# The factor of the MLP's norm moved into the last norm, and the residual's transposes and two up tiles moved in the order of PE

## What is computed

```python
def rmsnorm(x, g):
    x32 = x.astype(jnp.float32)
    y = x32 * lax.rsqrt(jnp.mean(x32 * x32, axis=-1, keepdims=True) + EPS)
    return y.astype(x.dtype) * g
...
        x = x + rmsnorm(merged @ w_out[l], post_norm_mix[l])
        h2 = rmsnorm(x, pre_norm_mlp[l])
        y = jnp.square(jax.nn.relu(h2 @ w_up[l])) @ w_down[l]
        x = x + rmsnorm(y, post_norm_mlp[l])
```

## Time and profile before

| | |
|---|---|
| Three runs | 1450.80, 1450.85, 1452.98 us; median 1450.85 |
| Span of the profiled execution | 1447.7 us (its own time is not given apart) |
| PE busy | 1319.0 us, 91% |
| DVE busy | 952.2 us, 66% |
| ACT busy | 493.1 us, 34% |
| POOL busy | 459.2 us, 32% |
| HBM | 274 GB/s over the span |

### The profile page before, as it was taken

One profiled execution on the slowest core, in us unless ns is written; L12 is line 12 of the kernel. 1 busy time (PEld: TensorE's weight loads), 2 busy tenths in 40 slices (PEclk: granted clock), 3 DMA queues, 4 the chain that ended last, 5 costly groups with the idle time before them and its releaser, 6 DMA issues.

```text
span 1447.7 us, 25101 instructions
## 1 busy us (share of the span) xinstructions
PE 1319.0 (91%) x9618; PEld 1240.8 (86%) x9618; DVE 952.2 (66%) x2094; ACT 493.1 (34%) x965; POOL 459.2 (32%) x325
## 2 busy tenths in 40 slices
PE   9999999999999896887878787879899999899997
PEld 8999999988889896887868787878886789789996
DVE  4689987665685775859585768755416447656665
ACT  5534456444133121212112221211225456434343
POOL 1587722000225554554545454546003000000000
PEclk9999999999999998898999999989999999999999
DMA  7555554553489999999999999999930134245552
GB/s 286 196 186 175 182 187 163 179 193 131 183 341 394 426 427 428 427 428 428 428 427 426 426 426 427 427 428 427 405 148 30 35 112 177 101 147 196 182 189 73
DMA packets 57896, 397.92 MB, mean 275 GB/s; under 512 B 6352, under 2 KB 9040, under 8 KB 10192
## 3 DMA queue, kind: packets, MB, share of 16 engines
q0 software_dynamic: 36864, 268.45, 44.1%
q1 hardware_dynamic: 20944, 128.28, 24.8%
HBM read 395.66 MB, written 1.05 MB: 274 GB/s over the span
## 4 chain that ended last, share of the span: by engine, by line
PE 57%; DMA 21%; DVE 11%; issue 7%; ACT 3%; POOL 1%; DVEq 0%; POOLq 0%; ACTq 0%
DMA rows_late<-peer_uv_dram,stage 21%; PE bank L745 11%; PE bank L746 11%; PE bank L747 11%; PE bank L1006 7%; PE bank L712 6%; PE bank L730 5%; DVE rows_late L2064 3%; ACT w_hi L1228 1%; POOL rows_late L654 1%; PE bank L867 1%; DVE w_lo L542 1%; PE bank L891 1%; PE bank L961 1%; PE bank L850 0%
## 5 line engine op out<-in xcount | busy, mean ns | idle before, releaser
L1006 PE MATMUL bank<-h_norm,rows_late 128*128 128x128 f32 x2816 | 327.8, 279 | 22.9 <-ACT h_norm L1417 22.9
L1006 PEld LDWEIGHTS bank<-h_norm,rows_late 128*128 128x128 f32 x2816 | 323.9, 195 | 26.0 <-ACT h_norm L1417 26.0
L2064 DVE SCALAR_TENSOR_TENSOR rows_late<-rows_late,squares 128x1024 f32<-128x1024 f32 x176 | 213.4, 1229 | 118.0 <-DMA rows_late<-peer_uv_dram,stage 107.9
L1006 PE MATMUL bank<-h_norm,rows_early 128*128 128x128 f32 x1280 | 174.3, 303 | 78.2 <-ACT h_norm L1417 78.2
L1006 PEld LDWEIGHTS bank<-h_norm,rows_early 128*128 128x128 f32 x1280 | 168.6, 217 | 84.1 <-ACT h_norm L1417 83.7
L654 POOL DMA_INDIRECT rows_late<-peer_uv_dram,stage x165 | 195.3, 1184 | 131.4 <-PE bank L1006 84.0
L542 DVE TENSOR_TENSOR w_lo<-raw,w_hi 128x2048 fp32r<-128x2048 f32 x66 | 151.3, 2294 | 100.5 <-ACT w_hi L1228 97.0
L1228 ACT ACTIVATE w_hi<-raw 128x2048 fp32r<-128x2048 f32 x94 | 178.9, 1904 | 56.4 <-PE bank L747 49.4
L745 PE MATMUL bank<-x_hi_a,w_hi 128*128 128x256 f32 x672 | 190.9, 284 | 2.7 <-DVE x_lo_a L1633 1.8
L746 PE MATMUL bank<-x_lo_a,w_hi 128*128 128x256 f32 x672 | 190.2, 283 | 0.0
L747 PE MATMUL bank<-x_hi_a,w_lo 128*128 128x256 f32 x672 | 190.1, 283 | 0.0
(11 more groups left out here) (353 smaller groups left out, 1886.1 us busy)
## 6 DMA issues: line engine op xcount, KB each, us to landing
raw<-w_in_dram SPq DMA_DIRECT2D x28, 1024.0 KB, 4.9
raw<-w_up_dram SPq DMA_DIRECT2D x16, 1024.0 KB, 4.9
raw<-w_down_dram SPq DMA_DIRECT2D x16, 1024.0 KB, 4.8
rows_late<-w_in_dram SPq DMA_DIRECT2D x10, 1024.0 KB, 12.7
raw<-w_kv_dram SPq DMA_DIRECT2D x8, 1024.0 KB, 4.9
rows_late<-w_peer_q_dram SPq DMA_DIRECT2D x5, 1024.0 KB, 11.8
raw<-sc_w_out_dram SPq DMA_DIRECT2D x4, 1024.0 KB, 4.9
raw<-cf_w_pw_dram SPq DMA_DIRECT2D x4, 1024.0 KB, 5.0
```

Source lines behind the costliest of these rows:

```text
L1006: mm = nc.tensor.matmul(ct(Y_ACC[c][t // 4], t % 4, P), expert_rows(k)[:, D + t * P:D + (t + 1) * P], ct(diag, k % DIAGS, P), start=False, ...
L2064: w_.scalar_tensor_tensor(out=row, in0=row, scalar=1.0, in1=h_tok[:, c * D:(c + 1) * D], op0=ALU.mult, op1=ALU.mult, accum_out=pre[:, side ...
```

## The change

Three things. First, the norm's factor r of a token leaves the up product. max(u, 0) without r, squared, is smaller by r², so is y, and the last norm divides it out again, save for its epsilon: y·r²/sqrt(mean(y²)·r⁴ + EPS) = y/sqrt(mean(y²) + EPS/r⁴). EPS/r⁴ is EPS·(m + EPS)² with m the mean square of the token. ACT computes it as one Square of the statistic (`up_eps`), and it stands as the bias where the last norm had EPS. The statistic is now taken by token, two single columns, with `squares` as the stationary operand. Square root, reciprocal and the multiplication by `rstd` are gone; `turns` is a plain max. Second, X stands behind U2 instead of ahead of D0, and ACT copies it out behind `hid_hi` 5 instead of 3. Third, U15 stands ahead of D13, and the list of loads ends up 13, down 12, up 14, up 15, down 13, down 14, down 15; the `w_hi` and `w_lo` of the last block come behind those of hidden tile 31. Three new columns (`eps_cubed_root`, `up_eps`) are allocated ahead of the large buffers, which lie 64 bytes further on.

```diff
@@ -80,6 +80,9 @@
+
+DOWN_BEHIND = {0: (), **{b: (b - 1,) for b in range(1, FH - 2)}, FH - 2: (), FH - 1: (FH - 3, FH - 2, FH - 1)}
@@ -155,11 +158,10 @@
         add("w_up_2", [b], "up", 2, "dve", 2 * b)
-        if b == 1:
+        if b == 2:
             other("xtok", 4, "act")
-        if b:
-            p.append(("w_down_2", b - 1, [], "dve"))
-    p.append(("w_down_2", FH - 1, [], "dve"))
+        for d in DOWN_BEHIND[b]:
+            p.append(("w_down_2", d, [], "dve"))
@@ -239,7 +241,7 @@
-SCALED = ("xa", "mlp")
+SCALED = ("xa",)
@@ -290,6 +292,8 @@
         eps_squared = sb("eps_squared", 1)
+        eps_cubed_root = sb("eps_cubed_root", 1)
+        up_eps = sb("up_eps", NC)
@@ -627,6 +631,7 @@
             g.memset(eps[:], EPS).then_inc(filled, 1)
+            g.memset(eps_cubed_root[:], EPS ** 1.5).then_inc(filled, 1)
@@ -782,7 +787,9 @@
                 pe.wait_ge(squared, square_count(name, k))
-                mm = nc.tensor.matmul(STAT[:, 0:SEQ], mean_d[:], ct(squares, k), start=(k == 0), stop=(k == DT - 1))
+                for c in range(NC):
+                    mm = nc.tensor.matmul(STAT[:, c:c + 1], ct(squares, k)[:, c * P:(c + 1) * P], mean_d[:, 0:1],
+                                          start=(k == c == 0), stop=(k == DT - 1 and c == NC - 1))
@@ -1158,21 +1165,32 @@
             linear("up", [3], "w_up_2", 1, "mlp", DT, 256, lo=P)
-            pe.wait_ge(residual_added, DT)
-            for n in range(4):
-                c, part = divmod(n, 2)
-                out = open_tile("xtok", n)
-                for j in range(4):
-                    mm = nc.tensor.transpose(out[:, j * P:(j + 1) * P], x_piece(c, 4 * part + j), ident)
-                mm.then_inc(acc_ready, 1)
-            pe.wait_ge(rooted, len(ROOTS))
-            for b in range(2, FH):
-                for f in (2 * b - 4, 2 * b - 3):
+            def down_pair(d):
+
+                for f in (2 * d, 2 * d + 1):
...
+
+            def x_by_token():
+
+                pe.wait_ge(residual_added, DT)
+                for n in range(4):
+                    c, part = divmod(n, 2)
+                    out = open_tile("xtok", n)
+                    for j in range(4):
+                        mm = nc.tensor.transpose(out[:, j * P:(j + 1) * P], x_piece(c, 4 * part + j), ident)
+                    mm.then_inc(acc_ready, 1)
+
+            pe.wait_ge(rooted, len(ROOTS))
+            for b in range(2, FH):
+                if b < FH - 1:
+                    down_pair(b - 2)
                 linear("up", range(2 * b, 2 * b + 2), "w_up_2", b, "mlp", DT, 256)
+                if b == 2:
+                    x_by_token()
+            down_pair(FH - 3)
@@ -1241,7 +1259,7 @@
                     if ROOTS[n - 1] in SCALED:
-                        wait_drained(act, {"xa": "q", "mlp": "up"}[ROOTS[n - 1]], 0)
+                        wait_drained(act, "q", 0)
@@ -1301,7 +1319,7 @@
-            act.wait_ge(filled, 6)
+            act.wait_ge(filled, 7)
@@ -1557,22 +1575,24 @@
             ahead("up", 0)
-            root("mlp")
+            act.wait_ge(stat_ready, NORM_AT["mlp"] + 1)
+            s.activation(up_eps[:], STAT[:, 0:NC], ACT.Square, scale=EPS ** 0.5, bias=eps_cubed_root[:, 0:1]).then_inc(rooted, 1)
...
                 s.activation(ct(hid_hi, f % FH), ct(hid, f % 4), ACT.Copy).then_inc(x_hi_ready, 1)
-                for n in range(4 if f == 3 else 0):
+                for n in range(4 if f == 5 else 0):
                     drain("xtok", n, ct(x_tok, n, 512), width=512)
-                round_to(LOAD_OF["up", 0] + f + 1)
+                round_to(LOAD_OF["up", 0] + f + (1 if f < 2 * FH - 2 else 0))
             act.wait_ge(acc_freed["act"], FREE_ORDER[TILE_AT["xtok", 3]][1])
+            act.wait_ge(rooted, len(ROOTS))
...
                 act.wait_ge(half_squared, c + 1)
-                s.activation(half_col[:, c:c + 1], sum_col[:, 2 * c:2 * c + 1], ACT.Identity, bias=eps[:, 0:1],
+                s.activation(half_col[:, c:c + 1], sum_col[:, 2 * c:2 * c + 1], ACT.Identity, bias=up_eps[:, c:c + 1],
@@ -2240,7 +2260,7 @@
             ahead("up", 0)
-            rstd_of("mlp")
@@ -2253,13 +2273,14 @@
                     dve.wait_ge(x_lo_ready, split_count("hid", f - 4))
-                dve.wait_ge(*freed(w_.scalar_tensor_tensor(out=turns[:], in0=acc("up", f), scalar=0.0,
-                                                           in1=rstd[:], op0=ALU.max, op1=ALU.mult)))
+                dve.wait_ge(*freed(w_.tensor_scalar(turns[:], acc("up", f), 0.0, None, ALU.max)))
...
                     hid_low(f - 1)
-                subtract_to(LOAD_OF["up", 0] + f + 1)
+                if f < 2 * FH - 2:
+                    subtract_to(LOAD_OF["up", 0] + f + 1)
             hid_low(2 * FH - 1)
+            subtract_to(len(LOADS))
```

## The result

| | us |
|---|---|
| before, median of 4 runs | 1450.82 (1449.55 to 1452.98) |
| changed, median of 4 runs | 1457.07 (1455.85 to 1457.46) |
| ratio, 95% interval | 1.0039 (1.0027 to 1.0052) |
| span of the profiled execution, changed | 1453.9 (its own time 1455.85) |

The changed kernel is 0.4% slower where 1447.4 was forecast. The last stage went as forecast; the loss stands ahead of it. Three marks, first before, then changed (PE timeline: start, us, instruction, idle before), show this: the first product behind the gather (`squares,rows_late`), the first up matmul (`x_hi_b,w_hi`) and the last matmul (`w_hi,hid_lo`). The other lines of the changed kernel are used further down.

A forecast was written before the change was run, and what follows sets the result against it. It took PE to bound the last stage, with DVE barely keeping up; -4.8 (reordering and norm factor) - 0.6 (end) + 2.0 (low clock) = -3.4 us took the span from 1447.7 to 1444.3, plus 3.15 gives 1447.4, range 1445.0 to 1450.3.

The forecast's parts named there:

- The step that failed: Large buffers, gather: 64 bytes off a multiple of 256 cost nothing, as `x_res` 383 and `cf_acc` 384 GB/s seemed equal.
- Rival (3): Gather: the 64-byte shift makes its packets 1% longer, costing 6.4 us, 1453.8 in all; chance 0.08.
- the rule named beside it: Skill's rule for descriptors off 256 bytes: 258 beats for 256 per 8 KB row, 0.8% on the gather, 1452.5 in all.
- The norm factor: Start of last stage: reciprocal goes, DVE's first run is 1.78 us earlier, plain max takes 0.42 us.
- D0 and U2 ahead of X: Start of last stage: first down pair at 1260.5, wait before fourth transpose group shrinks from 4.71 to 3.5 us; 4.8 gained.
- The clock: Behind the 3.5 us wait before the fourth transpose group: low PE clock costs 2.0 us, bounds 0 and 2.9.
- The statistic's new shape: PE, start of last stage: tile 3 ends at most 1.6 us later, hidden, costed at nothing.
- the two beats of 5.39: DVE, start of last stage: two tiles of 5.39 us put `turns` 5 at 1276.52.
- The end: Last pairs: wait for `hid_lo` (2.64 us) becomes one of 2.2 us for `w_lo`; 0.6 us gained.
- a possible loss of 1 to 1.7 us: Last pairs: if the wait at the end lowers PE's clock in a run, 1 to 1.7 us are lost.
- The sum of the stage: Last stage: -4.8 - 0.6 + 2.0 = -3.4 us.
- Rival (4): Last stage: reordering does nothing since PE waits for DVE anyway; only the reciprocal counts, -1.8 us, 1449.1; chance 0.06.

The follow-up runs named there:

- c5: Kernel before with only `rows_late`, `w_hi`, `w_lo` and other buffers behind the pad 64 bytes further on, `rows_early` aligned: 1447.70 us, ratio 0.9994.
- a4: Kernel before with `rows_early`, later small buffers and hid 64 bytes further on, `rows_late`, `w_hi` and `w_lo` unmoved: 1447.26 us, ratio 0.9990.
- c1: Kernel before with every large buffer 32 bytes past a multiple of 256: ratio 1.0080.
- c2: Kernel before with every large buffer 128 bytes past a multiple of 256: ratio 1.0082.
- d1: Kernel before with only `x_hi_a` and `x_lo_a` moved, 64 bytes further on: 1446.19 us, ratio 0.9965.
- d2: Kernel before with only `x_hi_a` and `x_lo_a` moved, 128 bytes further on: 1447.16 us, ratio 0.9978.
- d4: Changed kernel realigned to 256, residual transposes behind the second down pair, down 14 its own pair, both activation pairs 64 bytes further on: 1428.62 us, ratio 0.9843 to before.
- a2: Kernel before with all large buffers 64 bytes further on, nothing else: 1457.69 us, ratio 1.0059.
- b1: Kernel before with the new norm factor alone, both old orders kept, large buffers on multiples of 256: 1448.99 us, ratio 0.9986.
- c4: Changed kernel on multiples of 256 with the old order at the end: 1448.53 us, ratio 0.9982 to before.
- b2: Changed kernel on multiples of 256 with the residual transposes behind the second down pair: ratio 0.9933 to before.
- a1: Changed kernel with `row_pad` cut from 64 to 48, large buffers back on multiples of 256: 1442.92 us, ratio 0.9964 to before.
- a3: Kernel before with all large buffers 256 bytes further on: 1448.87 us, ratio 0.9999.

## Why the prediction was wrong, and where it was right

**The step that failed** is the one that set the 64 bytes aside: "So an offset of 64 bytes shows no cost, and a fixed price for a row would weigh eight times as much there as in the 8 KB rows of the gather." Its second half holds: the price of a packet is nearly fixed, 5.6 ns on 46.0 in rows of 1 KB and 4.3 ns on 309.1 in rows of 8 KB, so it weighs some nine times as much in the short ones. Its first half is what failed: the price isn't paid at once, and the window of the earlier trace rows from 3.70 to 4.90 us lies in the part of `x_res` that doesn't pay yet. The price begins only after a while (c5, a4, `cf_acc` in a4), and the gather, with nothing but rows off their multiple, pays nearly all the time. The trace of before already had it: at 5.10 to 5.70 us, where the last of `x_res` lands, it moved

```profile
5.10:5.70 0.60, 0.00 (x0) 0.00 (x0) 0.07 (x1) 0.60 (x3) 0.00 (x0) 1.00 1.13 359
```

359 GB/s. Other packets are mixed in there, but the 1 KB packets alone tell: they take 46.0 ns each from 3.4 to 4.9 us, and 51.7 from 5.2 to 5.8, the two values of `cf_acc` on its multiple and off it. One window inside a transfer doesn't tell its rate. Rival (3) had place and cause right, with a chance of 0.08; it was priced at 1% where 1.4% was measured, and the rule named beside it gave 0.8%. By that rule the price would double from 32 to 64 bytes and again to 128, and c1 and c2 show that it doesn't. Put in at the size of its packets, 8.9 us, the forecast would have been 1447.4+8.9 = 1456.3 against 1457.07. That this comes so close is in part luck, as the next sum shows.

**Of the 10.05 us** ahead of the stage 7.8 are the gather (from 367.42 to 1047.54, 680.12 us, before; 369.65 to 1057.59, 687.94, now). 2.2 arose in the first 30 us of the profiled execution, and no term of the sum had them. They are the clock's. The trace records 1.00 from 4.00 us before, 0.50 from 7.41 and 1.00 again from 14.24; in the changed kernel its first record, 1.00, comes at 17.36. Ahead of it PE goes at half pace, though the windows show 1.00 there for want of a record: the four records of a statistic that took 0.50 us before the fall took 0.85 then, and in the changed kernel from the start (before, then changed):

```profile
6.95 0.50 PE L901 MATMUL bank<-mean_d,squares 128*128 128x1 f32 x4
7.80 0.85 PE L901 MATMUL bank<-mean_d,squares 128*128 128x1 f32 x4
```

```profile
7.79 0.85 PE L908 MATMUL bank<-mean_d,squares 128*128 128x1 f32 x4
```

It isn't the 64 bytes: a4, d1, d2 and d4 have their first record at 17.0 to 17.5 us too, while a2, c1 and c2, with all large buffers off their multiple, have it at 5.4 to 6.5. So one execution has it and another doesn't; of d1's five runs the profiled one alone was 2.4 us above the rest. In all, 7.8 and 2.2 us stand in place of the 8.9, and the stage gained 0.4 more than forecast: 1447.4+7.8+2.2-0.4 = 1457.0.

**The norm factor**: right. `turns` 0 follows `w_lo`, the plain max takes 0.42, and b1 moves X by 1.75 us. The statistic's new shape (four records in 0.50 us) ends tile 3 0.2 us later, hidden behind PE's wait for `hid_lo`.

**D0 and U2 ahead of X**: right. D0 at 1270.67 is 1260.5+10.05 within 0.1, and the fourth group at 1287.04 is 1276.99+10.05 exactly; the wait is 3.62 (forecast 3.5), put down to `turns`.

```profile
1286.57 0.42 DVE L2276 TENSOR_SCALAR turns<-bank 128x256 f32<-128x256 f32 x1
```

This `turns` 5 is what the two beats of 5.39 gave, 1276.52+10.05.

**The clock**: it fell to 0.50 for 3.4 us, and cost less than taken. D1 starts at 1287.77, and U3 at 1294.63, 6.86 us later instead of 5.47. That is 1.4 us, and 0.1 in the group of X before it, for the 2.0.

**The end**: right. The wait for `w_lo` is 2.09 (forecast 2.2), and c4 puts the new end at 0.49 us (forecast 0.6). What the prediction kept as a possible loss of 1 to 1.7 us happened in the traces of b1, b2, c2, c5 and d1, at 1.6 us.

**The sum of the stage**: -3.8 us in the changed kernel and in a1 (193.24), forecast -3.4. Without the shift the change gains: a1's ratio of 0.9964 is 5.2 us (3.2 to 7.2) below before. Its trace has a gather 2.7 us shorter, within what kernels at 427 GB/s differ by.

**Rival (4)** fell: the norm factor moves X by 1.8 us in b1 (2.2 us in the stage, with the 1.6 of the low clock at its end added back), so the reordering gave some half of the stage's 3.8 us.

## What to carry to other kernels

Before a change that allocates anything, list where each large buffer starts, and pad so that what long transfers fill stays on a multiple of 256 bytes: here three columns, 12 bytes, moved everything by 64, and cost twice what the change gained. To tell a rate from a window, take windows at the start and at the end of the transfer, and compare packets of one size. When buffers move, count PE's matmuls in a window where it is busy throughout: where its two operands lie against each other was worth 2% either way here. And where a wait of some 2 to 4 us stands ahead of dense matmuls, put ready work into it rather than shorten it: the two waits left by this change were worth 7.85 us, twice the change itself.

## What the runs showed of the hardware

Transfers into SBUF places off a multiple of 256 bytes run at full rate at first. In rows of 8 KB a packet then takes 313.4 ns instead of 309.1 at offsets of 64 and 128 bytes and 314.3 at 32; in rows of 1 KB 51.5 to 51.8 instead of 46.0 at all three, which is 9% of the rate in a4. So the price is some 4 to 6 ns a packet, whatever its size and its offset.

PE's pace depends on where moving and stationary operand lie against each other: 0.120 us for a matmul of 256 columns where both start on a multiple of 256 bytes, 0.118 with the moving one 64 bytes further on, ratios of 0.9965 and, with both pairs, 0.9843 against 0.9913. With both moved together it is 0.120 again (a2). For 512 columns no layout here is faster, and one with the stationary operand 64 bytes further on is slower: 5.60 us a down pair instead of 5.47 (a4). The Trainium skill (TensorE: Matmul & The Clock Gate, Step-by-step: what each phase is for) says that the two operands have read ports of their own, so that loading weights takes nothing from the running matmul. That wouldn't lead one to expect a pace that depends by 2% on how the two lie. Whether the ports make it no run shows, and why 128 bytes help less than 64 is open.

The same wait of 2.1 to 2.7 us in the last pairs was followed by a clock of 1.00 in the traces of before, changed, a1, a2, a3, a4, c1, c4 and d2, and by 0.50 for 3.4 us in b1, b2, c2, c5 and d1. From the wait's end to the last matmul are 9.4 us in the first (9.6 in a4) and 11.0 in the second. So such a wait is a risk rather than a fixed price: its length alone doesn't decide (2.64 us in before, c2 and d1). The clock differs at the start in the same way: full speed is on record from 4.0 to 6.5 us on in thirteen traces, from 17.0 to 17.5 in five (changed, a4, d1, d2, d4), which costs some 2 us.
